# Two of three u blocks by high and low halves in three passes instead of plain fp32

## The reference, cut to what matters

```python
idx = jnp.take_along_axis(cand_i, pos, axis=-1)
g = jax.nn.softmax(top_s, axis=-1)
u_sel = jnp.take(u_tab, idx, axis=0)
h = jnp.einsum('bthkd,btd->bthk', u_sel, xb)
a = (jax.nn.gelu(h.astype(jnp.float32)) * g).astype(xb.dtype)
return jnp.einsum('bthk,bthkd->btd', a, jnp.take(v_tab, idx, axis=0))
```

## Time and profile before

| what | us |
|---|---|
| median of 3 runs (1537.07 to 1542.85) | 1540.49 |
| the profiled execution | 1540.41 |
| its span in the trace | 1538.6 |
| u stage, first c of it to c = 33 | 853 to 944 |
| u stage, the rest | 944 to 1224 |
| w stage | 1229 to 1532 |

### The profile page before, as it was taken

How to read it: one execution, slowest core, us unless ns; L and a number is a source line. 1 busy time by engine, 2 the same in 40 slices (tenths; PEclk the granted TensorE clock), 3 DMA queues, 4 the chain that set the end, 5 groups by cost and what they waited for, 6 DMA issues and landing times.

```text
span 1538.6 us, 26335 instructions
## 1 busy us (share of the span) xinstructions
PE 1510.0 (98%) x10162; PEld 1390.0 (90%) x10162; DVE 1106.3 (72%) x2153; ACT 766.1 (50%) x1562; POOL 334.5 (22%) x240
## 2 busy tenths in 40 slices
PE   6999999999999999999999999999999899999998
PEld 6999997799999977899999999999999877777777
DVE  6766678767666775656768895666666588988887
ACT  7554555555545555544444113444433356666665
POOL 1111113202111120100016010222222134343331
PEclk9999999999999999999999999999999999999999
DMA  5555556445555564344554477888888889999996
GB/s 187 185 187 182 184 182 220 140 138 165 186 185 183 174 197 144 127 148 135 174 175 124 155 279 242 290 287 299 292 293 296 279 280 343 341 335 327 350 339 214
DMA packets 95851, 344.68 MB, mean 224 GB/s; under 512 B 10664, under 2 KB 11952, under 8 KB 95728
## 3 DMA queue, kind: packets, MB, share of 16 engines
q1 hardware_dynamic: 77296, 275.89, 53.4%
q0 software_dynamic: 18432, 67.12, 12.3%
HBM read 341.92 MB, written 1.05 MB: 223 GB/s over the span
## 4 chain that ended last, share of the span: by engine, by line
PE 85%; DVE 6%; DMA 3%; ACT 3%; issue 2%; POOL 1%; SPq 0%; DVEq 0%; ACTq 0%; POOLq 0%
PE ps L1002 84%; DMA RAW<-wall 3%; DVE WL L434 2%; ACT WH L606 1%; DVE YS L1521 1%; DVE HL L1521 1%; POOL FS L520 1%; DVE XT L1518 0%; DVE SS L1521 0%; DMA XT<-xt 0%; PE ps L1158 0%; ACT HH L624 0%; POOL SM L487 0%; DVE MX L1712 0%; PE ps L1177 0%
## 5 line engine op out<-in xcount | busy, mean ns | idle before, releaser
L434 DVE TENSOR_TENSOR WL<-RAW,WH 128x1024 fp32r<-128x1024 f32 x361 | 442.1, 1225 | 188.2 <-ACT WH L606 167.9
L606 ACT ACTIVATE WH<-RAW 128x1024 fp32r<-128x1024 f32 x354 | 373.0, 1055 | 257.3 <-PE ps L1002 243.3
L1002 PE MATMUL ps<-XT,RAW 128*128 128x192 f32 x2048 | 344.1, 327 | 0.1
L1002 PEld LDWEIGHTS ps<-XT,RAW 128*128 128x128 f32 x2048 | 331.5, 190 | 0.5 <-issue 0.4
L1002 PE MATMUL ps<-HH,WH 128*128 128x256 f32 x976 | 279.9, 287 | 0.3 <-DVE WL L434 0.3
L1002 PE MATMUL ps<-HL,WH 128*128 128x256 f32 x976 | 276.1, 283 | 0.0
L1002 PE MATMUL ps<-HH,WL 128*128 128x256 f32 x976 | 275.9, 283 | 0.0
L1002 PE MATMUL ps<-WH,GG 128*128 128x512 f32 x768 | 267.5, 400 | 5.0 <-DVE GG L1518 4.6
L1002 PE MATMUL ps<-WL,GG 128*128 128x512 f32 x512 | 203.8, 398 | 0.0
L1002 PEld LDWEIGHTS ps<-HH,WH 128*128 128x128 f32 x976 | 186.8, 191 | 2.9 <-issue 2.4
L1002 PEld LDWEIGHTS ps<-HL,WH 128*128 128x128 f32 x976 | 187.0, 192 | 1.0 <-issue 1.0
(11 more groups left out here) (271 smaller groups left out, 2449.3 us busy)
## 6 DMA issues: line engine op xcount, KB each, us to landing
RAW<-wall SPq DMA_DIRECT2D x510, 512.0 KB
B<-rel SPq DMA_DIRECT2D x4, 768.0 KB, 6.0
DEC<-con SPq DMA_DIRECT2D x4, 384.0 KB, 4.3
XT<-xt SPq DMA_DIRECT2D x4, 256.0 KB, 5.6
UB<-utab,IDXU POOLq DMA_INDIRECT x64
VB<-wall,IDXV POOLq DMA_INDIRECT x64, 8.1
WIN<-con SPq DMA_DIRECT2D x1, 768.0 KB, 8.6
out<-XT SPq DMA_DIRECT2D x2, 256.0 KB, 2.6
```

Of the source, the lines that this page charges most:

```text
L434: ins = eng.tensor_tensor(wl, RAW[:, b % NRAW, :], wh.bitcast(F), ALU.subtract)
L606: act.activation(halves(b)[0], RAW[:, b % NRAW, :], ACT.Copy).then_inc(s_hi, 1)
L1002: return pe.matmul(o, l, r, start=start, stop=stop, skip_group_check=True)
```

## The change

A set `THREE` of u blocks leaves `DIRECT`. These get a high half on ScalarE and a low half on VectorE, and TensorE takes them by `block` with XH and XL, the halves of the 192 dense columns of the normed activations. ScalarE makes XH, one copy of 192 columns after each of the last eight pq blocks, and POOL makes XL after its last low halves. XH and XL lie in the place of VB, so the gathers of v (w) rows, three of which were made early, now all wait until the last block of THREE is done. VectorE's low of block c + 2 is moved behind the one-hots and the dot.

```diff
-DIRECT = set(range(UP, WP))
+THREE = {UP + c for c in range(36, 124) if c % 3}
+DIRECT = set(range(UP, WP)) - THREE
...
-            UB, VB = sb("UB", [128, NGET, D], F, ph), sb("VB", [128, NGET, D], F, ph)
+            UB = sb("UB", [128, NGET, D], F, ph)
+            with ExitStack() as sub:
+                XH, XL = sb("XH", [128, KD, ND], R, sub), sb("XL", [128, KD, ND], R, sub)
+            VB = sb("VB", [128, NGET, D], F, ph)
...
                 low_if_mine(b + 2)
+            for k in range(KD):
+                pool.wait_ge(s_hh, 48 + k + 1)
+                pool.tensor_tensor(XL[:, k, :], XT[:, k, DENSE], XH[:, k, :].bitcast(F), ALU.subtract).then_inc(s_hl, 1)
             candidates(0)
             candidates(1)
             pool.wait_ge(s_idx, 4)
-            for j in range(NGET):
+            for j in range(NSP):
                 gather_u(j)
-            for j in range(NGET):
-                gather_v(j)
-            for j in range(NGET, NSP):
-                gather_u(j)
-            for j in range(NGET, NSP):
+            pool.wait_ge(s_blk, max(THREE) + 1)
+            for j in range(NSP):
                 gather_v(j)
...
+                if l >= 8:
+                    act.wait_ge(s_xn, 8)
+                    act.activation(XH[:, l - 8, :], XT[:, l - 8, DENSE], ACT.Copy).then_inc(s_hh, 1)
...
-                    if UP + c + 2 >= WP:
+                    if UP + c + 2 not in DIRECT:
                         high(UP + c + 2)
...
-                direct(UP + c, bank[4 + (c + 1) % 2][:, 0:ND])
+                if UP + c in DIRECT:
+                    direct(UP + c, bank[4 + (c + 1) % 2][:, 0:ND])
+                else:
+                    block(UP + c, bank[4 + (c + 1) % 2][:, 0:ND], XH, XL, 48 if UP + c == min(THREE) else None)
...
                 gated(c - 1)
-                low_if_mine(UP + c + 2)
                 if c in QUAD_AT:
                     one_hots(QUAD_AT[c])
                 if c in DOT_SLOT:
                     dot(DOT_SLOT[c])
+                low_if_mine(UP + c + 2)
```

## The result

The changed kernel takes 1561.88 us (median of 4 runs, 1561.1 to 1563.86), the kernel before 1539.63 us beside it: ratio 1.0145, 95% interval [1.0123, 1.0168], so 22 us or 1.4% slower. Forecast were 1573 us, a range of 1548 to 1608, and slower with 0.88. The profiled execution took 1561.56 us.

What follows compares the result with a forecast made beforehand. The prediction took TensorE, its matmuls busy 98% of the core's time, as the bound. Its terms, 8.2 + 3 + 20 + 2 = +33 us on 1540.4, gave 1573 us, range 1548 to 1608.

Steps and rivals of the forecast that it cites:

- weight loads, 58 blocks: TensorE's u blocks: 24 fp32r records of 0.113 us replace 16 of 0.161, +8.2 us (ends 5.4 and 16.6).
- turns fp32 to fp32r: TensorE going from plain fp32 to fp32r blocks: 30 turns at 0.1 us, +3 us (ends 0 and 3).
- ScalarE's queue and RAW: u stage: high halves and their RAW waits delay weighted one-hots, so gates wait, +20 us (ends +8 and +56).
- XH, XL, the move of low: Making XH on ScalarE and XL on POOL, and moving VectorE's low: all costed at nothing.
- v gathers: Turn to the w stage: three later gathers compete with first w tiles for DMA, +2 us (ends 0 and +5).
- kind A: u stage, 16 quads with c = 2 mod 3, block c three-pass: 0.9 us each, 14 us (ends 4 and 34).
- kind B: u stage, 16 quads with c = 0 mod 3, block c plain: 0.4 us each, 6 us (ends 4 and 22).
- the signs named: Expected in the profile after: among others, TensorE idle before OHS matmuls near 20 us, VectorE's busy time up 71 us.
- 1 (the queue does not matter): Rival, ScalarE in the u stage: only the records count, +5 to +14 us, 1546 to 1554; chance 0.11.
- 2 (columns set the pace): Rival, TensorE: 192-column records go by columns, 0.0825 us each, making the kernel faster, -13 us, 1527; chance 0.06.
- 3 (four passes under 256 columns): Rival, TensorE: fp32r under 256 columns streams in four passes like plain fp32, +298 us, 1838; chance 0.04.
- 4 (VectorE full): Rival, u stage: VectorE's slot overflows, or landings near 8 us rule, more than +75 us, above 1615; chance 0.04.

Runs made afterwards that it cites:

- e2: The changed kernel with its 58 blocks given no high or low halves, TensorE using the last pq block's halves instead; 1546.13 us, ratio 1.0021 to the kernel before.
- e5: The kernel before, all u blocks plain, with all v gathers waiting until u block 122 is done; 1542.59 us, ratio 1.0014 to the kernel before.
- e1: The changed kernel with ScalarE taking a quad's weighted one-hots before the high half of block c + 2; 1547.88 us, ratio 1.0032 to the kernel before.
- e4: The changed kernel with 41 other blocks, whose high halves fall into ScalarE slots without a quad; 1545.32 us, ratio 1.0016 to the kernel before.
- e9: The changed kernel without 61 of its 64 gathers of u rows; 1553.80 us, ratio 1.0092 to the kernel before.
- e7: The changed kernel with VectorE's low half put back ahead of the one-hots and the dot; 1559.56 us, ratio 1.0119 to the kernel before.
- e6: e1 with three-pass blocks of 192, 96 and 48 columns; 1560.09 us in one execution, the kernel before 1540.56 us.
- e11: e10 with all 58 blocks instead of 29; 1566.94 us, ratio 1.0167 to the kernel before.
- e10: The changed kernel with 29 blocks, high weights loaded once for XH and XL side by side, weighted one-hots before gelu and high; 1534.01 us, ratio 0.9951 to the kernel before.

## Why the prediction was right, and where its sizes were off

| step | forecast | measured |
|---|---|---|
| weight loads, 58 blocks | +8.2 us | 58 x (24 x 0.112 - 16 x 0.161) = +6.5; 4.4 net (e2) |
| turns fp32 to fp32r | +3 | 0 |
| ScalarE's queue and RAW | +20 | 14 (spans), 15 (c = 34 to 124), 17 (ratios) |
| XH, XL, the move of low | 0 | 0 |
| v gathers | +2 | +2.2 (e5) |
| the whole | +33 | +22 (+21.0 by spans) |

No term was too small by more than 0.2 us, so no error made good another. The measured values come from different runs and views and add up only roughly.

**Weight loads.** The floor held, 0.112 for 0.113 us. Net it costs less: 4.4 us between c = 34 and c = 124 in e2's trace; e2 less e5 is 1.0 us by the ratios, with intervals that leave up to about 3. What gives back is next to the blocks: in e1 the 12 gate loads take 0.83 us behind the plain block shown and 0.69 behind the three-pass one (31 of the 48 quads stand behind a three-pass block). Over the 48 quads the gates' loads are busy 36.8 us in the kernel before and 34.2 in e1, and the gaps between them shrink by 2 us. Why they run closer was not tried.

```profile
1098.77 0.83 PEld L1009 LDWEIGHTS ps<-OHS 128*128 128x128 bf16 x12
...
1105.01 0.69 PEld L1009 LDWEIGHTS ps<-OHS 128*128 128x128 bf16 x12
```

**Turns.** This term had no substance. The matmuls after a turn are spaced as in the earlier trace rows:

```profile
1116.92 2.81 PE L1009 MATMUL ps<-XT,RAW 128*128 128x192 f32 x16
1119.44 0.39 PE L1009 MATMUL ps<-XH,WH 128*128 128x192 f32 x1
1119.66 0.28 PE L1009 MATMUL ps<-XL,WH 128*128 128x192 f32 x1
```

but the first of them starts 2.52 us after the sixteen of the plain block began, not 2.57 to 2.60. The gap of 0.22 behind it is an early start before it, not lost time. The weight loads say the same: in the changed kernel the first load of a three-pass block comes 2.55 us after that of the plain block ahead of it (13 cases with no gates between), and in the kernel before the next plain block comes after the same 2.55 us (45 cases). A spacing should be read over the whole group on both sides.

**ScalarE's queue.** The mechanism was right in both its parts and its place, shown by e1 (order), e4 (place) and e9 (landings). Its size was 3 to 6 us too large, and that is kind A: idle time of 10.3 us before its gates where 14 were forecast, against 6.3 and 6 for kind B. Kind A's tiles, the first of the pair, land in 3.9 us (median of the 15 of 29 whose landing is on record), not the 4.7 taken, and its high halves wait for RAW 0.5 us on average, not 0.8. The 4.7 us and the lateness of kind B were choices between wide ends (+8 to +56 in sum), so that the total came as near is in part luck.

**Gathers, low, XH and XL** came out as costed: the first u block's first load is at 852.75 us in the changed kernel and 852.64 before, and e5 and e7 stand for the other two. Of the signs named, the idle time before the gates stands in kinds A and B alone (0.1 us before the other 16 quads), and VectorE's low halves are busy 70.7 us more, 512.8 against 442.1 in the earlier trace rows.

**Rivals.** 1 (the queue does not matter) fell to e1; 2 (columns set the pace) and 3 (four passes under 256 columns) fell to e6 and to the spacing of 0.112 us at 192 columns. The Trainium skill (TensorE: Matmul & The Clock Gate, LDWEIGHTS) gives a load P/1.2 ns, 107 ns for 128 weight columns, with no term for the streamed ones; the 0.112 us at 48 and at 192 columns agrees. The 82.5 ns of rival 2 came from a formula that the same page (Back-to-back issue gap) gives for the isolated matmul and calls too low at small N, as it was here. By its section Weight-path perf modes, fast weight load is on when the number of weights is 128 and the input is not FP32. On fp32r it is not seen here: the loads last 0.19 us like those of plain fp32, those of bf16 0.097. 4 (VectorE full) was not this kernel, but it is e11.

## What to carry to other kernels

Count weight loads before counting columns: at 192 columns three passes take 3 x 0.112 = 0.336 us where the plain fp32 matmul took 2 x 0.161 = 0.322, and fewer columns made the passes no cheaper. One load for both halves of the activations, in 29 blocks and with the weighted one-hots first, is what turned the loss into a gain. When an instruction that waits for a transfer is put into an engine's queue, ask which short, urgent instruction stands behind it; here changing the places of two lines was worth 1.1%, two thirds to three quarters of the whole loss. And an engine that is busy for 87% of a stretch (e11's VectorE, 236.84 of the 272 us from 944 to 1216) can already hold up the others, once its results are on the way to the bound engine from two sides.

## What was not expected of the hardware

TensorE's granted clock fell in e6, though matmuls and loads followed without a gap. Windows of e6 (length, busy us of PE, PEld, DVE, ACT, POOL, granted clock, DMA share, GB/s):

```profile
950.00:980.00 30.00, 30.00 (x253) 29.86 (x252) 23.76 (x55) 18.04 (x50) 7.12 (x6) 0.90 0.83 305
...
1130.00:1160.00 30.00, 30.00 (x277) 29.85 (x276) 26.61 (x57) 18.47 (x57) 7.81 (x7) 1.00 0.85 298
```

0.90 to 0.94 from 950 to 1130 and 0.96 to 1.00 after it, where the changed kernel had 1.00 from 944 to 1216 with all columns streamed. Between the two levels of 2.4 and 1.2 GHz that is 12 to 20% of the time at the lower. Only blocks of 96 and 48 columns had been put in place of those of 192; the plain blocks' loads rose from 190 to 201 ns, c = 34 to c = 124 took 14.1 us more than in e1, and the run took 1560.09 us where e1 took 1547.88. A TensorE that is busy 100% by its records did not keep the full clock. The chip alone is not the reason, since e10 and e11 ran on the same one at 1.00 in this stage. This is one run, and what it takes was not tried further. The rows of 192 and 48 columns above, from 1109 to 1112, lie in a stretch at the full 2.4 GHz.
